# Where a kernel's tensors lie in SBUF: a pad of 128 bytes ahead of the activations, on one core of Trainium2

## The reference, cut to what matters

```python
def reference(x, mem, positions, ...):
    x = first_block(x, mem, positions, ...)     # mixer, cross attention, conv FFN (D_FF 2816)
    return second_block(x, c_2, ctx_2, ...)     # two layers, each with two SwiGLU FFNs (D_FF 2752)

def _conv_ffn(h, w_up, conv_w, w_down):
    u = _causal_dwconv(jnp.matmul(h, w_up), conv_w)
    gate, val = jnp.split(u, 2, axis=-1)
    return jnp.matmul(jax.nn.silu(gate) * val, w_down)

def swiglu(h, w_gu, w_down):
    gate, up = jnp.split(h @ w_gu, 2, axis=-1)
    return (jax.nn.silu(gate) * up) @ w_down

def adaln(cvec, w_mod, b_mod):
    m = jax.nn.silu(cvec) @ w_mod + b_mod       # 9 rows of 1024 per layer
```

## Time and profile before

| | |
|---|---|
| time, median of 3 runs | 2138.51 us (2137.96 to 2138.54) |
| the profiled execution's own time | 2140.59 us |
| its span, first to last instruction | 2138.8 us |
| instructions | 31174 |
| TensorE busy (matmuls) | 2071.4 us, 97% of the span |
| VectorE, ScalarE, GpSimd busy | 52%, 38%, 11% |
| mean granted clock of TensorE | 0.990 |
| read from HBM | 314 MB, 147 GB/s |

### The profile page before, as it was taken

The page is one execution under the profiler, slowest core; times in us unless marked ns, Lnnn a source line. Parts: engine busy times, 40 slices in busy tenths (PEclk is TensorE's granted clock), DMA queues, the critical chain, the costliest instruction groups (busy, mean ns, idle before and its releaser), DMA issues.

```text
span 2138.8 us, 31174 instructions
## 1 busy us (share of the span) xinstructions
PE 2071.4 (97%) x13450; PEld 1810.1 (85%) x13450; DVE 1115.4 (52%) x1486; ACT 821.4 (38%) x1049; POOL 224.9 (11%) x185
## 2 busy tenths in 40 slices
PE   6988999999999999999999999999999999999998
PEld 6985998999988888888888888888888888769998
DVE  6768555767643654454554532254464335645444
ACT  5742454655532222243342122234222225345344
POOL 1000000413111001100101001111100110001011
PEclk9999999999999999999999999999999999999999
DMA  6425654454642543342343432244343223364543
GB/s 239 158 80 177 218 197 178 147 180 171 212 177 74 192 158 116 121 180 98 118 171 132 150 110 82 89 163 138 133 162 138 100 88 109 110 243 162 180 173 106
DMA packets 54138, 317.08 MB, mean 148 GB/s; under 512 B 6000, under 2 KB 12400, under 8 KB 23792
## 3 DMA queue, kind: packets, MB, share of 16 engines
q1 hardware_dynamic: 50848, 308.99, 40.8%
q10 hardware_dynamic: 3152, 6.10, 0.8%
HBM read 314.01 MB, written 1.05 MB: 147 GB/s over the span
## 4 chain that ended last, share of the span: by engine, by line
PE 87%; DVE 6%; ACT 4%; issue 2%; DMA 0%; SPq 0%; POOL 0%; DVEq 0%; ACTq 0%; POOLq 0%
PE psum L276 27%; PE psum L277 26%; PE psum L278 26%; PE psum L1704 2%; ACT w_hi L252 2%; DVE w_lo L260 1%; PE psum L1311 1%; PE psum L1301 1%; DMA raw<-in_w_in_r 0%; PE psum L1325 0%; PE psum L913 0%; DVE xn_lo L1875 0%; PE psum L914 0%; DVE work L449 0%; DVE work L1018 0%
## 5 line engine op out<-in xcount | busy, mean ns | idle before, releaser
L276 PE MATMUL psum<-xn_hi,w_hi 128*128 128x256 f32 (+1 forms) x2600 | 862.9, 332 | 19.8 <-DVE xn_lo L456 9.8
L277 PE MATMUL psum<-xn_lo,w_hi 128*128 128x256 f32 (+1 forms) x2600 | 852.5, 328 | 0.0
L278 PE MATMUL psum<-xn_hi,w_lo 128*128 128x256 f32 (+1 forms) x2600 | 852.3, 328 | 0.0
L260 DVE TENSOR_TENSOR w_lo<-raw,w_hi 128x2048 fp32r<-128x2048 f32 (+1 forms) x246 | 510.8, 2077 | 401.9 <-ACT w_hi L252 401.0
L276 PEld LDWEIGHTS psum<-xn_hi,w_hi 128*128 128x128 f32 x2600 | 496.5, 191 | 72.9 <-issue 24.0
L277 PEld LDWEIGHTS psum<-xn_lo,w_hi 128*128 128x128 f32 x2600 | 496.8, 191 | 43.2 <-issue 1.2
L278 PEld LDWEIGHTS psum<-xn_hi,w_lo 128*128 128x128 f32 x2600 | 496.5, 191 | 41.9
L252 ACT ACTIVATE w_hi<-raw 128x2048 fp32r<-128x2048 f32 (+1 forms) x246 | 421.5, 1714 | 168.8 <-PE psum L278 158.2
L276 PE MATMUL psum<-h_hi,w_hi 128*128 128x512 f32 (+1 forms) x913 | 311.9, 342 | 1.6 <-POOL h_lo L1649 1.6
L278 PE MATMUL psum<-h_hi,w_lo 128*128 128x512 f32 (+1 forms) x913 | 310.8, 340 | 0.0
L277 PE MATMUL psum<-h_lo,w_hi 128*128 128x512 f32 (+1 forms) x913 | 310.8, 340 | 0.0
(11 more groups left out here) (378 smaller groups left out, 1387.0 us busy)
## 6 DMA issues: line engine op xcount, KB each, us to landing
raw<-in_mod SPq DMA_DIRECT2D x72, 1024.0 KB, 4.8
raw<-in_a_up SPq DMA_DIRECT2D x42, 1024.0 KB, 4.8
raw<-in_b_up SPq DMA_DIRECT2D x42, 1024.0 KB, 4.8
raw<-in_ffn_up SPq DMA_DIRECT2D x22, 1024.0 KB, 4.9
raw<-in_a_down SPq DMA_DIRECT2D x32, 704.0 KB, 4.1
raw<-in_b_down SPq DMA_DIRECT2D x32, 704.0 KB, 4.1
raw<-in_ffn_down SPq DMA_DIRECT2D x16, 704.0 KB, 4.1
raw<-in_wo SPq DMA_DIRECT2D x8, 1024.0 KB, 4.9
```

The lines of the kernel that those rows point to most:

```text
L260: dve.tensor_tensor(w_lo[:, slot, 0:size], raw[:, raw_slot(("main", g)), 0:size], w_hi[:, slot, 0:size].bitcast(F32), ALU.subtract).then_i ...
L276: pe.matmul(out, lh, rh, start=first, stop=False, skip_group_check=group)
L277: pe.matmul(out, lh, rl, start=False, stop=False, skip_group_check=group)
L278: return pe.matmul(out, ll, rh, start=False, stop=last, skip_group_check=group)
```

## The change

A tensor of 32 float32 (128 bytes) per partition that nothing uses is laid between `w_lo` and `xc`, and `mrow` is no tensor any more but columns 7680 to 7935 of `work`.

```diff
@@ -174,6 +174,7 @@
         raw = sb("raw", [P, SLOTS, CHUNK])
         w_hi = sb("w_hi", [P, SLOTS, CHUNK], F32R)
         w_lo = sb("w_lo", [P, SLOTS, CHUNK], F32R)
+        sb("between", [P, 32])
         xc = sb("xc", [P, KT, 2 * T])
         xn_hi = sb("xn_hi", [P, KT, 2 * T], F32R)
         xn_lo = sb("xn_lo", [P, KT, 2 * T], F32R)
@@ -192,7 +193,7 @@
         b_mod = sb("b_mod", [P, 144])
         c_in = sb("c_in", [P, KT, 2])
         c_pad = sb("c_pad", [P, KT, C_AT + 32])
-        mrow = sb("mrow", [P, 256])
+        mrow = work[:, 7680:7936]
         X = slice(0, T)
         C = slice(T, 2 * T)
         XC = slice(0, 2 * T)
```

## The result

The changed kernel takes 2161.59 us (median of 4, 2155.95 to 2161.96) against 2138.24 us (4, 2136.85 to 2138.54): a ratio of 1.0104, 95% interval 1.0093 to 1.0116. It is 23 us slower, where I had forecast 91 us less.

A forecast was written before the change was run, and what follows sets the result against it. TensorE's matmul pace was taken as the bound; 51 + 47 = 98 us, times 0.93, gave -91 us, so profiled 2140.6 became 2049.6 and the median 2047. Own range 2032 to 2075, chance 0.45; 8-in-10 range 2030 to 2142.

The forecast's parts named there:

- The step that failed: Three matmul passes: activation streams moved to multiples of 256 lose 32 wasted columns, at most 13.3 ns per matmul.
- the 216 ns at 512 columns: Forecast pace of 512-wide activation matmuls: 213.3 + 2.5 ns, down from 226.7, worth 51 us over 4725 matmuls.
- the 112 ns at 256: Forecast pace of 256-wide activation matmuls, limited by loading the next 128x128 matrix; from 120, worth 47 us over 5814.
- the 13 ns: Time of each activation-streaming matmul not belonging to its columns, whatever its width; 140 us over 10539 matmuls.
- the stream's term: Activations moved to multiples of 256 in the three passes: 98 us, times 0.93 gives -91 us; ends 0 and -130.
- rival C: Loaded and streamed operands at different halves of 256 bytes disturb each other: slower, up to +130 us, 2269; chance 0.10.
- the two small terms of 3 us: TensorE's 1.6 us wait for GpSimd's low part of the hidden tile, and the tables' 1.4 us; each taken as nothing.
- A: Rival: the rest is float32r's own, no start matters; each term 0, time 2138.5; chance 0.37 with the unmoved tensor.
- B: Rival: only 512-wide streams gain, loading from `w_hi` and `w_lo` holds 256-wide at 120; -47 us, 2091; chance 0.08.
- the tables: `ident`, `minus`, `rot` and `row_sums`, now 128 past a multiple: between nothing and 1.4 us, taken as nothing.
- the supply: ScalarE, VectorE and landings behind each 256-wide chunk keep up with a TensorE 7% faster; costed at nothing.
- the row buffer: Six copies of 417 ns and 24 loads and matmuls keep shapes, order and waits at its new place; taken as nothing.

The follow-up runs named there:

- e11b: Against the kernel before: split weights written 64 bytes later in their slot in the 256-wide stages, row buffer in `work`; 2128.07 us, ratio 0.9967.
- experiment one: Against the changed kernel: the 128-byte pad moved ahead of `raw`, so split weights and activations begin at multiples of 256; 2138.26 us, ratio 0.9998.
- e14: Against the kernel before: only stream operands moved against the weights, xn by 192 bytes and h by 16; 2146.9 us.
- e5: Against the kernel before: only stream operands moved against the weights, xn by 64 bytes and h by 192; 2143.4 us, ratio 1.0018 to 1.0042.

## Why the prediction was wrong

**What bounds the kernel** was read rightly: TensorE's pace, by the distance of starts, and only the part beyond the columns. The sum of the measured paces is +21.1 us for +21.2 of the span.

**The step that failed** is "If a stream is fetched from the multiple below its start, the 32 wasted columns go", and the argument ahead of it, that 13.3 ns are 32 columns are 128 bytes. That was a coincidence of one number. The run with weights and activations at multiples of 256 has the same 226.7 ns. No run shows the paces that the sum used: for the 216 ns at 512 columns, with 2.5 ns beyond the columns, the lowest measured was 226.7, and for the 112 ns at 256 it was 113.3 (e11b, in the last FFN). That the load sets a limit there stays an estimate, from L2082 in the kernel before, where steps of 111 ns go with a PEld that is busy 1.90 of 1.90 us (1005.4 to 1007.3). The 106.7 ns for 256 columns stand as an estimate, beside the 106.9 by which the two widths differ. In place of -98 us of pace the term measured +27.4 at 512 columns and -6.3 at 256: what the pad changed was the distance between loaded and streamed operand, from 0 to 128. In the kernel before all streams of activations in the three passes begin 128 bytes past a multiple; a match that nothing in the trace can vary deserved less than 0.45.

**Where the 13 ns come from** was not shown: that they belong to the fetch of the streamed operand was an estimate of mine. At the granted clock of 0.50 a 256-wide step takes 213.6 ns before and after, so the pad has no effect there, and if the columns take twice the estimated 106.9 ns, no rest is left either. Left out was the load. I had excluded it because plain float32 matmuls show little beyond their columns: seven of 256 columns take 1.68 less 0.38 us, 217 ns each, and six of 128 columns 0.83 less 0.275, 111 ns each. But there 128 more columns cost 106 ns, as much as 256 more in float32r, so they say nothing of a float32r stream at the granted clock of 1.00. In those experiment one shows that the place of the loaded operand acts on the pace, 232.5 ns against 226.7. What makes the 13 ns stays open: every distance tried keeps at least as much at 512 columns, and the two theories on it missed.

**The bounds of the stream's term** were drawn from nothing to a gain. Nothing excluded a loss, and rival C had named one; it belonged to the range, which ended at 2142. The forecast's own range was also summed wrongly: half of the 256-wide gain given back makes 2138.5 - 47 - 22 = 2069, not 2075, and all 98 landing makes 2040, with the two small terms of 3 us 2037, not 2032.

**The rivals.** C named the right cause, loaded and streamed operand at different halves of 256 bytes, with 0.10 (232.5 ns for 226.7 at 512 columns); that the two reads disturb each other was not shown. Its size was off: 5.8 ns at 512 columns and a small gain at 256, not 13.3 at each. A is wrong, since starts matter, though right in that multiples of 256 have no merit. B didn't occur; the 256-wide pace was not held by the load at 120, since e14 reaches 114.6.

**The small terms at nothing** were right: VectorE's and ScalarE's busy times, the tables (80 transposes in L1325 and 24 matmuls in L1718, hence the 104), the supply, and the row buffer (its own run: 0.9996).

## What to carry to other kernels

In this kernel, bound by TensorE with float32r streams at the granted clock of 1.00, the layout of SBUF is a parameter of the matmul's pace: a tensor of 128 bytes laid between loaded and streamed operands changed the 512-wide step from 226.7 to 232.5 ns and the time by 1% without an instruction changing, so compare the starts of both operands modulo 256 bytes before a difference is put down to anything else. Read the pace from the distance of starts, by width, and look whether it is even. Of two explanations that the trace cannot vary, neither earns a likely forecast, however well a number fits.

## What was not expected of the hardware

- The pace of 512-wide float32r matmuls at the granted clock 1.00 ranges from 226.7 to 234.3 ns by the distance between loaded and streamed operand. That of 256-wide ones ranges from 113.3 to 120.0, and there one distance can have two paces (113 and 118 in e5). Shifting both operands together by 128 bytes changes neither (226.7 and 119.8).
- Four bytes of distance cost as much as 16 or 32 (233.3 ns), eight less (228.9).
- Loading 64 columns in place of 128 in one of three passes, with 64 rows of output in place of 128, made the 512-wide steps longer, 229.8 for 226.7, and the 256-wide shorter, 116.8 for 119.8.
- At the granted clock of 0.50 the effect is not there: 213.6 ns a step of 256 columns before and after. Nothing is left beyond the columns either, if they take twice the 106.9 ns estimated at 1.00.

What in the hardware makes the table what it is stays open. No run shows a mechanism for it, nor for the even paces (226 and 227 ns) beside the uneven ones (228 to 241 in the changed kernel), nor for the two paces of one distance. Why 208 and 240 (226.8 ns) behave as 0 while 224 (233.3) doesn't is not explained.
